# A hybrid transformer step: the ACT queue's gate and rope loads put behind the first modulation weights, parameter loads reordered, one matmul dropped

## The chip, the cores and the metric

The kernel runs on one core of a Trainium2 chip. Its engines are TensorE (PE, with its weight loads shown as PEld), VectorE (DVE), ScalarE (ACT), GpSimd (POOL) and SyncE (SP); SP, ACT and POOL issue the DMA transfers, each on a queue of its own (q1 is SP's, q10 is ACT's, q0 is POOL's), and 16 DMA engines carry them. The metric is the device time of one execution in microseconds, as the median of several runs.

## The reference, cut to what matters

One inference step of a layer: 512 latent tokens and 128 context tokens with 1,024 features pass through an adaptive layer norm (modulation), one input projection, attention beside a gated linear recurrence (RG-LRU), an output projection and a mixture of 32 experts. The change touches the start of it only:

```python
def adaln(cvec, w, b):
    m = jax.nn.silu(cvec) @ w + b            # w: 1024 x 6144
    return six vectors: sh1, sc1, g1, sh2, sc2, g2

h = modulate(rms_norm(x, norm1), sh1, sc1)   # needs the first 2048 columns of w
z = h @ w_in                                 # q, k, v, xr (recurrence), gb (gelu gate)
xc = dw_conv(xr, conv_w, conv_b)             # width 4
r = sigmoid(xc @ wa[d] + ba[d])              # block-diagonal, 8 blocks of 64, two directions
i = sigmoid(xc @ wx[d] + bx[d])
# q and k are normed (q_norm, k_norm) and turned with rotary tables
```

## The kernel before

The program is written by hand, engine by engine: each engine has one list of instructions in order, and semaphores tie the lists together. No scheduler moves anything.

**Start.** SP issues the two conditioning vectors (line 352), the five blocks of tokens (line 354), and then, all on q1, in this order: the first halves of the columns of the eight row blocks of the first 2,048 columns of w_mod (`w_mod_columns(c, 0)`, line 358), a first part of w_in (`w_in(0)`, line 374), the second halves (`w_mod_columns(c, 1)`), `w_in(1)`, and, each behind a wait on PE's progress, `w_mod(8)` to `w_mod(11)` (line 363), `w_in(2)` and `w_in(3)`, four parts of the q/k/v columns (line 392), and `w_mod(12)` onwards. The pieces that a transfer is cut into have the length of a contiguous run: 2 KB for the halves of w_mod, 1 KB for the parts of w_in, 8 KB for `w_mod(8)` and later ones, 3 KB for the q/k/v columns.

**ACT at the start.** It loads the identity, three small parameters (norm1, conv_b, the first 2,048 entries of b_mod), waits for `par_c` and computes a tanh for SiLU, loads five more small parameters into rows of `prow` (tile q_hi_lo), squares the five token blocks for the RMS norm (line 527), loads b_mod for later groups (line 531), evicts transposed tokens (line 540), and then issues 13 transfers in a row: eight of the gate weights (line 554, 64 partitions x 4 runs of 64 floats each, so 256 runs of 256 bytes), two rotary tables (lines 556, 557), q_norm and k_norm broadcast to all partitions (lines 558, 559) and cached values (line 560). Its next work is `z_evict(0)` (line 574), which copies the first 128 recurrence columns out of PSUM.

**PE at the start.** Small warming matmuls (line 1410), `first_modulation(c, half)` (line 1397), the transpose of the parameter rows, which waits for all eight parameter loads (`par_in`, line 1413), and the transposes of the tokens (line 1373); then `mod_turn(0)` (line 1406), a single matmul of the identity whose result nobody reads (line 1425), and the projection `z(m, part)` (line 1464) in two halves of the contraction, because the second half needs the second halves of the modulation. The order from there is: z(0) first half, first_modulation(0,1) and (2,1), z(1,0) first half, first_modulation(4,1) and (6,1), z(1,1) first half, mod_turn(1), z(0) second half, modulation(8) and (9) (line 1385), z(1) second half, gates(0) (line 1439), modulation(10) and (11), z(2) and gates(1), z(3)..., gates(2), modulation(12) and (13), and so on. `gates(0)` waits for all eight gate loads (`gate_in`) and for `conv(0)` on DVE.

**DVE there.** modulate(1), then `conv(0)` (lines 936 and 938, waits for ACT's `z_evict(0)`), `rope_tables()` (lines 982 and 985, waits for the four transfers of `attn_in`, the tables and the two norms), `conv(1)`, `gates(0)` and `gates(1)` of the recurrence (lines 947 to 952), `conv(2)`.

The semaphore `wm_in[5]` counts the second halves of row blocks 4 to 7; at 64 all four have landed. PE waits for it before first_modulation(4,1).

Of the kernel before, what the change touches and what calls it, by code (L numbers as in the profile page):

```python
# [7 lines left out]
ACT = mybir.ActivationFunctionType  # L8
# [8 lines left out]
P = 128  # L17
# [33 lines left out]
WIDE = 4 * 512  # L51
# [14 lines left out]
R_CTX, R_C, R_N1, R_CB, R_CW, R_BA, R_BX, R_LAM, R_ST, R_BM, ROWS = 0, 8, 16, 24, 28, 44, 52, 60, 68, 76, 92  # L66

C_SSQ, C_RSTD, C_HALF, C_TH, C_KAP, C_BA, C_BX, C_LRU, C_MS2, C_RS2, C_KAP2 = 0, 5, 10, 20, 36, 44, 52, 60, 100, 105, 110
# [8 lines left out]
def build(nc, a):  # L77

    with ExitStack() as ctx:
        def sb(name, shape, dt=F32, c=ctx):  # L80
            return c.enter_context(nc.sbuf_tensor(name, shape, dt))

        def sem(name):
            return ctx.enter_context(nc.semaphore(name))


        X = sb("x_tok", [P, NT, D])
        HM = sb("hT_mixT", [P, DC, TOK])
        ident = sb("ident", [P, P])
        par = sb("par_cols", [P, ROWS])  # L90
        mcol = sb("mod_cols", [P, 2, 2, DC])
        csil = sb("silu_c", [P, DC, 32])
        small = sb("small", [P, N_SMALL])
# [12 lines left out]
        final = sb("final_step", [P, 1], U32)  # L106
        count = sb("count_ones", [P, 2, P], F16)
        tab = sb("routing_table", [P, sum(n for _, n in TABLE)])
        logit = sb("logits", [P, NT, NG + NE])
        W1 = sb("w1", [P, DC * D])  # L110
# [41 lines left out]
        ps = ctx.enter_context(nc.psum_tensor("ps", [P, 8, 512], F32))  # L152
# [9 lines left out]
        prow = qhl[:, 0, :]  # L162
# [22 lines left out]
        def temp(c, lo, n):  # L185

            return HM[:, NT + c, lo:lo + n]
# [11 lines left out]
        runs, reps, start = temp(2, 40, NE), temp(2, 72, PAIRS), temp(2, 88, PAIRS + 1)  # L199
# [47 lines left out]
        wm_in = [sem(f"wm_in{i}") for i in range(6)]  # L247
# [262 lines left out]
        def _(act):  # L510
# [1 line left out]
            rows = lambda v: v.rearrange("(c p) -> c p", p=P)  # L512
            act.dma_start(ident[:, :], a["k_ident"]).then_inc(S["ident_in"], 16)

            for v, r in ((a["norm1"][0], R_N1), (a["conv_b"][0], R_CB), (a["b_mod"][0, 0:WIDE], R_BM)):
                n = v.shape[0] // P
                act.dma_start(prow[r:r + n, :], rows(v)).then_inc(S["par_in"], 16)
            act.wait_ge(S["par_c"], 1)
            act.activation(small[:, C_TH:C_TH + 16], par[:, 0:16], ACT.Tanh, scale=0.5).then_inc(S["csil"], 1)
            for v, r in ((a["conv_w"][0], R_CW), (a["lru_ba"][0], R_BA), (a["lru_bx"][0], R_BX),  # L520
                         (a["lru_lambda"][0], R_LAM), (a["state_lru"][0, 0], R_ST)):
                n = v.shape[0] * v.shape[1] // P
                act.dma_start(prow[r:r + n, :], v.rearrange("k (c p) -> (k c) p", p=P)).then_inc(S["par_in"], 16)

            for t in range(NT):
                act.wait_ge(rows_in[t], 16)
# [17 lines left out]
            def mod_out(g):  # L544

                act.wait_ge(S["mod_ev"], g + 2)
                for v in range(2):
                    act.dma_start(a["mod_rows"][v, g * WIDE:(g + 1) * WIDE].rearrange("(q n) -> q n", q=4),
                                  msb[v:v + 97:32, :]).then_inc(S["mod_out"], 16)
            act.wait_ge(S["cleared"], 4)  # L550
            for k, w in enumerate((a["lru_wa"][0], a["lru_wx"][0])):
                for d in range(2):
# [73 lines left out]
            for m in range(1, LC):  # L626
                gates(2 * m - 1)
                z_evict(m + 1)
                roots(m - 1)
                gates(2 * m)  # L630
            mod_out(1)
            z_evict(LC + 1)
            gates(UNITS - 1)
# [4 lines left out]
            q_out(0)  # L638
            squares(2)
            mod_out(2)  # L640
            q_out(1)
            squares(3)
# [11 lines left out]
            for n in range(N + 8):  # L654
# [7 lines left out]
                if n < N:  # L662
                    if n >= 3:
# [3 lines left out]
                                   scale=SCALE, bias=sm[:, 1, n:n + 1], accum_out=sm[:, 2, n:n + 1]).then_inc(S["prob"], 1)  # L667
# [695 lines left out]
        def _(pe):  # L1363
# [38 lines left out]
            def mod_turn(half):  # L1402

                pe.wait_ge(S["mod_ev"], half + 1)
                for b in range(4):
                    ins = pe.matmul(ps[:, 7, 4 * b:4 * b + 4], msb[:, b * P:(b + 1) * P], pairsum, start=True, stop=True)
                ins.then_inc(S["mrow_t"], 1)
# [14 lines left out]
            first_modulation(6, 0)  # L1422
            x_turn(4)
            mod_turn(0)
            pe.matmul(ps[:, 5, :], ident[:, :], X[:, 0, 0:512], start=True, stop=True)

            def gates(u):
                m, d = u // 2, u % 2
# [128 lines left out]
            for n in range(N + 7):  # L1557
# [19 lines left out]
                if n < N:  # L1577
# [6 lines left out]
                    for lo, k, bank in ((0, HALF, b), (HALF, HALF, b + 1)) if t < LT else ((KEYS, CTX, b),):  # L1584
                        for s in range(2):
                            ins = pe.matmul(ps[:, bank, 0:k], qs[:, h, t * P:(t + 1) * P], ks[:, g, s, lo:lo + k],  # L1586
                                            start=(s == 0), stop=(s == 1))
# [13 lines left out]
                if 0 <= m < N:  # L1601
# [6 lines left out]
                    for i in ((0, 1), (2,), (3,), (4,))[part]:  # L1608
                        if i not in kt:
                            continue  # L1610
                        for e in range(2):
# [4 lines left out]
                                            start=(i == 0), stop=(i == kt[-1]))  # L1616
# [73 lines left out]
            for t in range(NT):  # L1690
                for k in range(TOP):
                    ins = pe.matmul(ps[:, 4, 0:COLS], slotp[:, t, k, :], hit[:, t, k, :],
                                    start=(t == 0 and k == 0), stop=(t == NT - 1 and k == TOP - 1))
# [58 lines left out]
            for t in range(NT):  # L1752
                for k in range(TOP):
                    ins = pe.matmul(ps[:, 5, 0:PARTS * COLS], slot1[:, t, k, :],
                                    step1w[:, t * TOP + k, :, :].rearrange("p s n -> p (s n)"),
                                    start=(t == 0 and k == 0), stop=(t == NT - 1 and k == TOP - 1))
# [25 lines left out]
            for t in range(NT):  # L1782
# [4 lines left out]
                for half in range(2):  # L1787
                    if t in PE_SUMS:
                        pe.matmul(ps[:, 2 * t % 8 + half, :], ident[:, :], y0[:, t, half * 512:(half + 1) * 512],
                                  start=True, stop=False)  # L1790
# [63 lines left out]
```

## Time and profile before

| | us |
|---|---|
| median of 3 runs | 632.55 |
| runs | 631.70, 632.55, 633.89 |
| the profiled execution | 631.70 |
| its span, first to last instruction | 629.5 |
| PE busy in it | 595.7 (95%) |
| DVE busy | 352.2 (56%) |
| ACT busy | 177.5 (28%) |
| POOL busy | 94.4 (15%) |
| DMA q1 / q10 / q0, share of 16 engines | 63.1% / 2.4% / 7.1% |

The span is what the profile shows of the execution; the rest of its time lies around it. Busy shares are averages over very different stages: in the first 70 us the DMA engines are busy without a break and PE is fed by them, from 80 to 370 us PE sets the pace, and the experts (from 370 us on) share it between PE and the stream of expert weights.

### The profile page before, as it was taken

To read this page: it belongs to the slowest core of one execution; us is meant where nothing else is said; L and a number is where in the kernel's file an instruction comes from. 1 tells how busy PE (TensorE), PEld (TensorE's weight loads), DVE (VectorE), ACT (ScalarE), POOL (GpSimd) and SP (SyncE) were. 2 spreads that over 40 slices of the span, in tenths; PEclk is the share of its full clock that TensorE was granted. 3 is DMA by queue.
4 is the path that set the end of the run, shared out by engine and by line. 5 is a ranking of instruction groups with operands and counts; after the bars stand their busy time and mean duration, and the time that the engine had idled before them with its cause. 6 is when DMAs were issued, how large, how long until landed. Compare 5 with 4: busy or idle time off the path is not lost.

```text
span 629.5 us, 9459 instructions
## 1 busy us (share of the span) xinstructions
PE 595.7 (95%) x3311; PEld 332.8 (53%) x3312; DVE 352.2 (56%) x786; ACT 177.5 (28%) x369; POOL 94.4 (15%) x131
## 2 busy tenths in 40 slices
PE   4989999999998999999999989999999999789797
PEld 2534455555666677645555445555555555355453
DVE  2747798765664887655666773333334333313347
ACT  4203887601144777721111101100110110011110
POOL 4000011122161000000000111212122121201200
PEclk9999999999999999999999899999999999979999
DMA  8999833330039639539114949999999999999877
GB/s 320 369 363 382 321 148 134 140 133 2 0 89 281 242 95 278 222 107 394 67 68 173 383 172 389 420 418 416 421 418 413 417 421 421 418 423 415 357 261 290
DMA packets 48129, 176.23 MB, mean 280 GB/s; under 512 B 10972, under 2 KB 18152, under 8 KB 34400
## 3 DMA queue, kind: packets, MB, share of 16 engines
q1 hardware_dynamic: 36848, 154.86, 63.1%
q0 software_dynamic: 6688, 15.58, 7.1%
q10 hardware_dynamic: 4560, 5.35, 2.4%
q8 instruction: 21, 0.34, 0.2%
q14 instruction: 12, 0.10, 0.0%
HBM read 163.31 MB, written 21.14 MB: 293 GB/s over the span
## 4 chain that ended last, share of the span: by engine, by line
PE 73%; DMA 13%; SPq 7%; DVE 4%; issue 1%; ACT 1%; POOL 1%; POOLq 0%; DVEq 0%; ACTq 0%
PE ps L1731 16%; PE ps L1548 11%; PE ps L1464 9%; PE ps L1747 7%; PE ps L1476 6%; DMA expert_w<-exp_w_up 5%; PE ps L1586 4%; PE ps L1613 4%; SPq L358 3%; PE ps L1595 3%; DMA w_mod_ring<-w_mod 2%; SPq L329 2%; DMA w<-w_mod 2%; PE ps L1439 2%; PE ps L1699 2%; PE ps L1385 2%
## 5 line engine op out<-in xcount | busy, mean ns | idle before, releaser
L1731 PE MATMUL ps<-expert_w,hT_mixT 128*64 128x256 f32 x1120 | 136.2, 393 | 11.4 <-DMA expert_w<-exp_w_up 11.1
L1731 PEld LDWEIGHTS ps<-expert_w,hT_mixT 128*64 128x64 f32 x1120 | 84.2, 136 | 66.8 <-issue 22.9
L1464 PE MATMUL ps<-hT_mixT,w 128*128 128x128 f32 (+1 forms) x256 | 72.6, 437 | 1.2 <-DVE hT_mixT L913 1.2
L1548 PE MATMUL ps<-w,hT_mixT 128*128 128x512 f32 x160 | 71.9, 597 | 0.0
L1747 PE MATMUL ps<-expert_w,w 128*64 128x512 f32 x280 | 65.8, 598 | 0.0
L736 ACT ACTIVATE w<-ps 128x128 f32<-128x128 f32 x36 | 10.0, 278 | 193.0 <-PE ps L1731 193.0
L1299 DVE SCALAR_TENSOR_TENSOR w<-w,ps 128x128 f32<-128x128 f32 x36 | 10.4, 288 | 86.7 <-ACT w L736 86.7
L1464 PEld LDWEIGHTS ps<-hT_mixT,w 128*128 128x128 f32 x256 | 38.9, 191 | 35.8 <-issue 32.6
L1317 DVE TENSOR_TENSOR w<-ps,w 128x1024 f32<-128x1024 f32 x18 | 22.1, 1225 | 59.9 <-PE ps L1747 59.9
L1476 PE MATMUL ps<-w_qkv,hT_mixT 128*128 128x512 f32 (+1 forms) x160 | 53.2, 488 | 0.2 <-DVE v_tok L1001 0.2
L1548 PEld LDWEIGHTS ps<-w,hT_mixT 128*128 128x128 f32 x160 | 29.1, 191 | 29.9 <-issue 29.7
L1476 PEld LDWEIGHTS ps<-w_qkv,hT_mixT 128*128 128x128 f32 x160 | 29.8, 190 | 22.1 <-issue 19.7
L1747 PEld LDWEIGHTS ps<-expert_w,w 128*64 128x64 f32 x280 | 19.0, 136 | 33.0 <-issue 30.8
L1077 DVE TENSOR_REDUCE softmax_stat<-ps 128x1 f32<-128x640 f32 (+1 forms) x40 | 28.6, 716 | 11.9 <-PE ps L1586 11.8
L1586 PE MATMUL ps<-k_stack,q_stack 128*128 128x320 f32 (+1 forms) x144 | 30.6, 331 | 3.2 <-ACT q_work L666 3.2
L829 POOL DMA_INDIRECT y_rows<-w,slot_row_now x17 | 23.9, 1407 | 55.9 <-DVE w L1317 53.3
L1586 PEld LDWEIGHTS ps<-k_stack,q_stack 128*128 128x128 f32 x144 | 21.2, 188 | 16.7 <-issue 11.5
L666 ACT ACTIVATE q_work<-ps,softmax_stat 128x640 f32<-128x640 f32 (+1 forms) x40 | 28.3, 708 | 4.3 <-DVE softmax_stat L1078 3.9
L661 ACT ACTIVATE w_qkv<-ps 128x640 f32<-128x640 f32 (+1 forms) x40 | 24.7, 618 | 14.5 <-PE ps L1595 14.2
L813 POOL DMA_INDIRECT w<-h_rows,slot_token_now x17 | 17.6, 1033 | 66.7 <-PE ps L1699 66.7
L1613 PE MATMUL ps<-w_qkv,v_tok 128*64 128x256 f32 x168 | 25.6, 400 | 0.0
L1595 PE MATMUL ps<-ident,q_work 128*128 128x128 f32 x168 | 25.2, 275 | 0.0
(287 smaller groups left out, 767.7 us busy)
## 6 DMA issues: line engine op xcount, KB each, us to landing
expert_w<-exp_w_down SPq DMA_DIRECT2D x31, 1024.0 KB, 19.2
expert_w<-exp_w_gate SPq DMA_DIRECT2D x29, 1024.0 KB, 14.8
expert_w<-exp_w_up SPq DMA_DIRECT2D x29, 1024.0 KB, 17.5
w_mod_ring<-w_mod SPq DMA_DIRECT2D x14, 1024.0 KB, 6.5
y_rows<-zero_rows POOLq DMA_DIRECT2D x10, 512.0 KB, 10.0
expert_w<-y_rows SPq DMA_DIRECT2D x10, 512.0 KB, 8.9
recurrence<-w_mod SPq DMA_DIRECT2D x8, 512.0 KB, 10.0
w<-w_in SPq DMA_DIRECT2D x4, 1024.0 KB, 16.7
```

The source lines that it names most:

```text
L661: act.activation(probT[:, m % HEADS, 0:k], wide[:, 4 * 512:4 * 512 + k], ACT.Copy).then_inc(S["pT_a"], 1)
L666: act.activation(probs(n), scores(n), ACT.Exp, scale=SCALE, bias=sm[:, 1, n:n + 1], accum_out=sm[:, 2, n:n + 1]).then_inc(S["prob"], 1)
L829: pool.indirect_dma_start(a["y_rows"], bass.IndirectOffsetOnAxis(pidc[:, 0:1], 0), y, None, bounds_check=TOP * TOK - 1, oob_is_err=False). ...
L1077: step(dve.tensor_reduce(sm[:, 0, n:n + 1], scores(n), AXY, ALU.max))
L1464: ins = pe.matmul(ps[:, bank, 0:n], w1v[:, c, m * P:(m + 1) * P], HM[:, c, lo:lo + n], start=(c == 0), stop=(c == DC - 1))
L1476: ins = pe.matmul(ps[:, bank, 0:n], HM[:, c, t * P:(t + 1) * P], wqv[:, c, lo:lo + n], start=(c == 0), stop=(c == DC - 1))
L1548: ins = pe.matmul(ps[:, 2 * (t % 2) + half, :], HM[:, c, t * P:(t + 1) * P], w1v[:, c, half * 512:(half + 1) * 512], start=(c == 0), stop= ...
L1586: ins = pe.matmul(ps[:, bank, 0:k], qs[:, h, t * P:(t + 1) * P], ks[:, g, s, lo:lo + k], start=(s == 0), stop=(s == 1))
L1595: ins = pe.transpose(ps[:, 4 + i // 4, (i % 4) * P:(i % 4 + 1) * P], prob[:, m % 3, i * P:(i + 1) * P], ident[:, :])
L1613: ins = pe.matmul(out.rearrange("p (b n) -> p b n", b=2), vt[:, i if t < LT else NT, g * HD:(g + 1) * HD], probT[:, 4 * g + e:4 * g + 4:2, ...
L1731: ins = pe.matmul(ps[r, 2 + k, 0:2 * P].rearrange("p (k f) -> p k f", k=2), xT[:, c, r], gate_up(i)[:, :, c, k:FF:FC], start=(c == 0), sto ...
L1747: ins = pe.matmul(ps[r, 5 + half, :].rearrange("p (a n) -> p a n", a=4), actT[:, c, r], down(i, c, half), start=(c == 0), stop=(c == FC - 1))
```

## The change

On ACT, the wait for `par_c` and the tanh come ahead of all parameter loads but the identity, and the 16 rows of b_mod come last of the eight parameter loads. Also on ACT, a wait for `wm_in[5]` to reach 64 is put ahead of the 13 transfers of gates, tables, norms and cached values. On PE, the single unread matmul behind `mod_turn(0)` is gone.

```diff
             act.dma_start(ident[:, :], a["k_ident"]).then_inc(S["ident_in"], 16)
 
-            for v, r in ((a["norm1"][0], R_N1), (a["conv_b"][0], R_CB), (a["b_mod"][0, 0:WIDE], R_BM)):
+            act.wait_ge(S["par_c"], 1)
+            act.activation(small[:, C_TH:C_TH + 16], par[:, 0:16], ACT.Tanh, scale=0.5).then_inc(S["csil"], 1)
+            for v, r in ((a["norm1"][0], R_N1), (a["conv_b"][0], R_CB)):
                 n = v.shape[0] // P
                 act.dma_start(prow[r:r + n, :], rows(v)).then_inc(S["par_in"], 16)
-            act.wait_ge(S["par_c"], 1)
-            act.activation(small[:, C_TH:C_TH + 16], par[:, 0:16], ACT.Tanh, scale=0.5).then_inc(S["csil"], 1)
             for v, r in ((a["conv_w"][0], R_CW), (a["lru_ba"][0], R_BA), (a["lru_bx"][0], R_BX),
                          (a["lru_lambda"][0], R_LAM), (a["state_lru"][0, 0], R_ST)):
                 n = v.shape[0] * v.shape[1] // P
                 act.dma_start(prow[r:r + n, :], v.rearrange("k (c p) -> (k c) p", p=P)).then_inc(S["par_in"], 16)
+            act.dma_start(prow[R_BM:ROWS, :], a["b_mod"][0, 0:WIDE].rearrange("(r p) -> r p", p=P)).then_inc(S["par_in"], 16)
...
+            act.wait_ge(wm_in[5], 64)
             act.wait_ge(S["cleared"], 4)
             for k, w in enumerate((a["lru_wa"][0], a["lru_wx"][0])):
...
             mod_turn(0)
-            pe.matmul(ps[:, 5, :], ident[:, :], X[:, 0, 0:512], start=True, stop=True)
```

ACT's list at the very start, before (q_hi_lo is the tile of the parameter rows, the names behind the arrow are the inputs; what an instruction waits for stands in brackets):

```order
L513 DMA ident<-k_ident 128x128
L517 DMA q_hi_lo<-norm1 8x128
L517 DMA q_hi_lo<-conv_b 4x128
L517 DMA q_hi_lo<-b_mod 16x128
L519 ACT_TABLE_LOAD
L519 ACTIVATE small<-par_cols 128x16 [waits par_c]
L523 DMA q_hi_lo<-conv_w 16x128
L523 DMA q_hi_lo<-lru_ba 8x128
L523 DMA q_hi_lo<-lru_bx 8x128
L523 DMA q_hi_lo<-lru_lambda 8x128
L523 DMA q_hi_lo<-state_lru 8x128
L527 ACTIVATE w_qkv,small<-x_tok 128x1024 [waits rows_in0]
```

The same place on ACT with the change:

```order
L513 DMA ident<-k_ident 128x128
L516 ACT_TABLE_LOAD
L516 ACTIVATE small<-par_cols 128x16 [waits par_c]
L519 DMA q_hi_lo<-norm 8x128
L519 DMA q_hi_lo<-conv_b 4x128
L523 DMA q_hi_lo<-conv_w 16x128
L523 DMA q_hi_lo<-lru_ba 8x128
L523 DMA q_hi_lo<-lru_bx 8x128
L523 DMA q_hi_lo<-lru_lambda 8x128
L523 DMA q_hi_lo<-state_lru 8x128
L524 DMA q_hi_lo<-b_mod 16x128
L528 ACTIVATE w_qkv,small<-x_tok 128x1024 [waits rows_in0]
```

Three loads moved from ahead of the tanh to behind it, b_mod to the end, all of them still ahead of the first square.

ACT's list at the 13 transfers, before (gate_w, rope, gain and v_tok are their tiles; xr_pad is what `z_evict` writes):

```order
L540 ACTIVATE hT_mixT<-ps 128x4x128 [waits xnT] x5
L554 DMA gate_w<-lru_wa 64x4x64 [waits cleared]
L554 DMA gate_w<-lru_wa 64x4x64 x3
L554 DMA gate_w<-lru_wx 64x4x64 x4
L556 DMA rope<-k_cos 128x256
L557 DMA rope<-k_sin 128x256
L558 DMA gain<-q_norm 128x64
L559 DMA gain<-k_norm 128x64
L560 DMA v_tok<-cache_v 128x128
L574 ACTIVATE xr_pad<-ps 128x512 [waits z_mm,cleared]
```

And with the change:

```order
L541 ACTIVATE hT_mixT<-ps 128x4x128 [waits xnT] x5
L556 DMA gate_w<-lru_wa 64x4x64 [waits cleared,wm_in5]
L556 DMA gate_w<-lru_wa 64x4x64 x3
L556 DMA gate_w<-lru_wx 64x4x64 x4
L558 DMA rope<-k_cos 128x256
L559 DMA rope<-k_sin 128x256
L560 DMA gain<-q_norm 128x64
L561 DMA gain<-k_norm 128x64
L562 DMA v_tok<-cache_v 128x128
L576 ACTIVATE xr_pad<-ps 128x512 [waits z_mm,cleared]
```

The order is the same; the first of the 13 now waits for wm_in5 too, and the other twelve and the eviction of xr_pad stand behind it.

## Rows read from the trace of the kernel before

**Rows 1.** Chain of work that ended last, 0 to 60 us: start, us, what.

```profile
24.30 13.91 DMA w<-w_mod
38.26 1.92 PE ps L1397 x16
...
58.16 14.30 DMA w_mod_ring<-w_mod
```

**Rows 2.** Timeline of PE, 24 to 73 us: start, us, line, shapes, [idle before <-releaser].

```profile
24.99 1.10 PE L1425 MATMUL ps<-x_tok,ident 128*128 128x512 f32 x2
26.27 4.56 PE L1464 MATMUL ps<-hT_mixT,w 128*128 128x512 f32 x16 [0.17 <-DVE hT_mixT L913]
38.26 1.06 PE L1397 MATMUL ps<-w_mod_ring,silu_c 128*32 128x512 f32 x8 [1.66 <-DMA w<-w_mod]
53.92 2.33 PE L1439 MATMUL ps<-xc,gate_w 128*128 128x512 f32 x8
72.50 1.06 PE L1385 MATMUL ps<-w_mod_ring,silu_c 128*32 128x512 f32 x8 [0.23 <-DMA w_mod_ring<-w_mod]
```

**Rows 3.** Timeline of ACT at its 13 transfers (ACTq: issuing) and z_evict(0).

```profile
24.33 2.69 ACTq L554 DMA_DIRECT2D gate_w<-lru_wa x4
27.05 3.80 ACTq L554 DMA_DIRECT2D gate_w<-lru_wx x4
30.88 1.57 ACTq L556 DMA_DIRECT2D rope<-k_cos x1
...
35.74 0.45 ACTq L560 DMA_DIRECT2D v_tok<-cache_v x1
46.91 0.60 ACT L574 ACTIVATE xr_pad<-ps 128x512 f32<-128x512 f32 x1 [21.99 <-PE ps L1464]
```

**Rows 4.** DMA queues, 28 to 36 us: packets, MB, share of 16 engines.

```profile
q10 hardware_dynamic: 1187, 0.29, 17.3%
```

**Rows 5.** DMA queues, 37 to 40 us.

```profile
q10 hardware_dynamic: 727, 0.18, 29.7%
```

**Rows 6.** DMA queues, 42 to 48 us.

```profile
q1 hardware_dynamic: 316, 2.33, 94.3%
q10 hardware_dynamic: 316, 0.15, 9.0%
```

**Rows 7.** DMA queues, 52 to 56 us.

```profile
q1 hardware_dynamic: 1356, 1.39, 108.5%
```

**Rows 8.** Tile gate_w: its two groups of issues, and all eight to landing.

```profile
L554 ACTq DMA_DIRECT2D gate_w<-lru_wx x4: 637/638/1797, 27.0 to 29.0; - x4
DMA to landing us min/median/max: 6.6/10.9/13.1
```

**Rows 9.** Tile gain: q_norm and k_norm, us from issue to landing.

```profile
DMA to landing us min/median/max: 14.8/15.7/16.6
```

**Rows 10.** Timeline of DVE, 48 to 68 us.

```profile
48.05 0.80 DVE L936 TENSOR_SCALAR xc<-xr_pad,par_cols 128x512 f32<-128x512 f32 x2 [2.60 <-ACT xr_pad L574]
52.04 0.43 DVE L982 TENSOR_TENSOR rope_k<-rope,gain 128x256 f32<-128x256 f32 x1
...
59.46 0.83 DVE L947 SCALAR_TENSOR_TENSOR q_work<-recurrence 128x640 f32<-128x640 f32 x1 [1.00 <-ACT recurrence L593]
67.07 0.82 DVE L947 SCALAR_TENSOR_TENSOR q_work<-recurrence 128x640 f32<-128x640 f32 x1 [5.19 <-ACT recurrence L593]
```

**Rows 11.** Windows: us, busy of PE, PEld, DVE, ACT, POOL, PEclk, DMA share, GB/s.

```profile
15.00:18.00 3.00, 3.00 (x15) 1.28 (x14) 2.87 (x6) 0.75 (x3) 0.00 (x0) 0.50 1.06 363
36.00:38.00 2.00, 0.60 (x2) 0.00 (x0) 0.00 (x0) 0.00 (x0) 0.00 (x0) 1.00 1.12 317
```

**Rows 12.** Timeline of ACT and PE, 5 to 15 us.

```profile
5.34 1.06 ACT L527 ACTIVATE w_qkv<-x_tok 128x1024 f32<-128x1024 f32 x1 [1.34 <-DMA x_tok<-x_sample]
10.77 1.06 ACT L527 ACTIVATE w_qkv<-x_tok 128x1024 f32<-128x1024 f32 x1
13.58 1.06 PE L1397 MATMUL ps<-recurrence,silu_c 128*32 128x512 f32 x8 [3.45 <-DMA recurrence<-w_mod]
```

## The prediction, on record before the change was run

> **What bounds the kernel now.** I read the chain of waits first. In the first 60 us it is fed by transfers: the last first-modulation matmuls start when the second halves of w_mod have landed at 38.26, and the next link that is a transfer is `w_mod(13)`, which takes the chain from 58.16 to 72.5 [rows 1]. PE's timeline says what each is worth: PE stood idle 1.66 us before 38.26 and 0.23 us before 72.50, and in between no other wait for a transfer is listed for it; it came to gates(0) at 53.92 and went straight on [rows 2]. From 72.5 to the end of attention PE lists no wait for a transfer, so a delay of PE there goes through to the end almost whole.
>
> Then the DMA queues by stretch. q1 (SP) and q10 (ACT) share the 16 engines, and they take turns piece by piece: from 42 to 48 us, when q1 carries the 8 KB pieces of w_mod(8) and later, both moved 316 pieces, 53 per us [rows 6]. When q1 carries 2 KB pieces, q10 gets 1,187 in 8 us, 148 per us [rows 4]; with the 1 KB pieces of w_in it gets 727 in 3 us, 242 per us [rows 5]. Alone, q1 moves 1,356 pieces of 1 KB in 4 us, 339 per us [rows 7]. So how fast ACT's small transfers get through is set by how long SP's pieces are at that moment. That decides this case.
>
> **The start of ACT (tanh first, b_mod last).** The tanh can come some 0.4 us earlier, but its reader, first_modulation, waits for w_mod until 13.58 [rows 12]: worth nothing. The three loads that moved behind it take about 1.2 us of issuing, so the first square starts near 6.6 instead of 5.34. The squares were held by token arrivals, so the last one moves from 10.77 by about 0.3 us only, and the normed tokens come 0.3 us later. PE waits for w_mod again right after the first transposes, and that absorbs it. b_mod's parameter rows would be issued near 6.4; with the 6.6 us of the quickest gate load [rows 8] they land by 13.0, ahead of PE's need at 14.64, where its first modulation ends [rows 12]. Cost 0; if that cover is gone, 0.3 us.
>
> **The unread matmul (line 1425).** With its group it takes 1.10 us at 24.99, and z(0) behind it waits for DVE's modulate until 26.27 anyway [rows 2]. Gain 0 to 0.1 us. It kept PE busy, so the clock is the risk: but the idle 1.66 us before 38.26 left the granted clock at 1.00 [rows 11], and the hole here would be 1.2 us. Taken as 0.
>
> **The wait for wm_in[5]: what it gives.** q10 held 17.3% of the engines over the 8 us from 28 to 36 [rows 4], 1.4 us, and some 0.1 more until the halves of w_mod were through. Without it they land near 38.26 - 1.5 = 36.8, and PE, free at 36.6, goes on 1.5 us earlier: first_modulation(4,1), z(0), modulation(8), (9) and z(1) all move up, and PE reaches gates(0) near 52.4.
>
> **What it costs, first the gate weights.** The 13 issues start at 36.8 instead of 24.33. The quickest gate load took 6.6 us to landing [rows 8], of which its 256 pieces and some 16 closing ones are 1.8 us at 148 per us [rows 4]; so beside a busy q1 the first piece moves some 4 us or a little more after the issue, here at about 41. What is q1 doing then? Behind the halves come the 1,024 pieces of w_in(1): at 339 per us, 3 us, they are through by about 38. Then come the 4 MB of w_mod(8) to (11) in 8 KB pieces, at 2.33 MB in 6 us [rows 6] 10 to 10.5 us, to about 48.5. In those 7.5 us q10 moves 7.5 x 53 = 400 pieces. The eight gate loads are 8 x 256 = 2,048 pieces and some 16 closing ones each, 2,176. The remaining 1,780 go beside the 1 KB pieces of w_in(2) and (3), at 242 per us: 7.3 us, to 55.8. With the last landing they are there at about **56.5**. In the run before they had a landing time of at most 13.1 us [rows 8] from issues that ended at 30.85 [rows 3], so were there by 42.
>
> **Second, ACT itself.** ACT needs its own list: z_evict(0) stands behind the 13 issues. Before, they took from 24.33 to 36.2, 11.9 us, and z_evict(0) was at 46.91, right when PE delivered [rows 3]. The first seven gate issues took 0.64 us each, the eighth 1.80 [rows 8], the tables 1.57 and about 1.4, the last 0.45 [rows 3]. I read this as a queue that takes no more than a certain stock: when the eighth was issued, from 29.0 to 30.85, seven had put 1,904 pieces in, and by my rate of 148 per us from 28.5 on some 75 of them had been moved at 29.0 and some 350 at 30.85. Lower bound: the same 11.9 us, ACT free at 48.7. Upper bound: the same stock, about 1,540 pieces before a new issue goes in; then the eighth issue waits until some 370 are moved (48), and the last until about 1,200 are moved (400 by 48.5, then 242 per us: 51.8), ACT free at 52.3. conv(0) follows the eviction (46.91 to 52.04 [rows 3, 10], 5.1 us), so it ends between 53.8 and **57.4**. I take the upper one, since it is the reading that explains the growing issue times.
>
> PE waits for both at gates(0). Two separate roads give 56.5 and 57.4; I take 57.2, against 53.92: +3.3 us. At 72.5 PE no longer waits for w_mod(13), whose bytes are the same in either program: -0.2. The 1.5 us won at 38 is inside this: it is lost at gates(0), and would be lost at 72.5 otherwise.
>
> **Third, the clock.** PE would be idle from 52.4 to 57.2, 4.8 us. After the idle 3.45 us before 13.58 [rows 12] the granted clock was 0.50 from 15 to 18 [rows 11], in all some 3.4 us at the lower of its two levels (1.2 instead of 2.4 GHz). Work at that level loses half of its time: at most 1.7 us for one such stretch, none if it passes while PE still waits. I take 1.2.
>
> **Fourth, DVE.** q_norm and k_norm took 14.8 and 16.6 us to land [rows 9]. Now the four transfers of attn_in are 576 pieces behind the gates: near 60. DVE waits there in rope_tables, its own 2 us and conv(1) (4 us, as conv(0) [rows 10]) bring it to 66, and DVE's gates(0) moves from 59.46 to there. But before its next one DVE had 5.19 us idle at 67.07 [rows 10], and its need moves by 4 us as well: gates(1) near 71 finds DVE free at 68.5, and PE wants conv(1) only at gates(2), near 73. Taken as 0; bound 2 us.
>
> Sum: +3.3 - 0.2 + 1.2 = **+4.3 us** on the profiled execution: span 629.5 to 633.8, its time 631.70 to 636.0. The profiled one is 0.85 us under the median of the runs, so the median goes from 632.55 to **636.9**.
>
> **Rivals.** (a) Late, but mildly: ACT gets through in its old 11.9 us, the gate loads alone hold PE to 56.5, and the clock doesn't fall in work: +2.6 - 0.2 = +2.4, 635.0. For it: ACT's slow issues fell into a time in which SP's were held up too, so they may not count stock at all.
> (b) In time, and absorbed: q10 gets several small pieces for each long one of q1. With nine for one, 53 x 9 = 477 per us, 2,176 pieces would be through in 4.6 us, landed by 47; ACT is free by 45, PE runs through at 52.4 and then waits 1.7 us at 72.5 for w_mod(13). Change about 0, 632.4. Against it: 316 to 316. The Trainium skill (DMA: Bandwidth & Descriptors, section Queues, rings and completion order) says that an engine drains a whole packet, typically nine to seventeen descriptors, from one ring before it turns to the next. By that rule this rival would be the outcome; the counts of pieces here speak against it.
> (c) Faster: as (b), and w_mod(13) lands earlier too. Its mechanism is the tail of q1's stream: SP issues w_mod(12) and (13) on PE's progress (57 to 58), and if the landing at 72.5 hangs on the issue and not on the bytes ahead, all 1.5 us go through: 631.0. Against it: 14.3 us from issue to landing [rows 1] is a queue of bytes.
> (d) Much later, beyond 639.5: q10 starts later than 41, the clock falls twice, or DVE's delay reaches gates(2).
>
> **How the numbers follow.** Forecast 0.50 (635.3 to 639.5), (a) 0.17, (b) 0.17, (c) 0.07, (d) 0.09. From 632.0 to 639.5 lie the forecast, (a) and most of (b), 0.82. A change within 0.3%, 1.9 us, is about what a measurement can't tell from none. Slower by more: the forecast, (d) and most of (a), 0.73. Same: (b) and the rest of (a), 0.20. Faster: 0.07.
>
> **What would show it.** Right: PE starts first_modulation(4,1) at 36.6 to 37; the issues of the gate loads begin there and the last of the 13 ends near 52; z_evict(0) at 52 instead of 46.9; gates(0) on PE near 57, with a wait of 4 to 5 us for ACT/DVE or a gate load; granted clock 0.5 for some us behind it; DVE waiting for gain near 60; no wait at modulation(13). Wrong: q10 moving far more pieces per us than q1 between 41 and 48, or z_evict(0) at 45.4. If gates(0) starts by 54.5, the forecast falls.

## The result, and the profile after

| | before | changed |
|---|---|---|
| median, us | 632.55 (630.50 to 635.09, 6 runs) | 637.81 (637.21 to 638.93, 6 runs) |
| ratio, 95% interval | | 1.0083 [1.0057, 1.0108] |
| profiled execution, us | 631.70 | 639.40 |
| its span | 629.5 | 637.4 |

The changed kernel is 5.3 us slower. Its profiled execution lies 1.6 us above its own median, so its rows show a little more than the change costs; the kernel was run once more later, beside three of the experiments: 636.80 us, 1.0077 [1.0050, 1.0105].

ACT's timeline of the changed kernel, 24 to 55 us (start, us, line, tiles, and in brackets the idle time before and what ended it), answers to [rows 3]:

```profile
37.53 2.68 ACTq L556 DMA_DIRECT2D gate_w<-lru_wa  x4
40.24 9.56 ACTq L556 DMA_DIRECT2D gate_w<-lru_wx  x4
49.83 0.79 ACTq L558 DMA_DIRECT2D rope<-k_cos  x1
...
52.66 0.49 ACTq L562 DMA_DIRECT2D v_tok<-cache_v  x1
53.25 0.77 ACT L576 ACTIVATE xr_pad<-ps 128x512 f32<-128x512 f32 x2 [26.53 <-DMA w_mod_ring<-w_mod]
```

The 13 issues take 15.6 us for 11.9 before. The last four gate issues take 5.8 us more than before, all of it in two of them, and the five issues behind them 2.0 us less. z_evict(0), at 46.91 before, is at 53.25. The chain of waits shows the two issues apart, and what follows them (start, us, what):

```profile
25.07 12.44 DMA w<-w_mod
...
40.91 3.05 ACTq L556
43.99 5.02 ACTq L556
49.03 10.13 DMA gate_w<-lru_wx
59.21 4.03 PE ps L1440 x8
```

In [rows 1] the path runs from w_mod's halves into PE's own work; now it runs through ACT's issues into the landing of the last gate load. PE's timeline, beside [rows 2]:

```profile
28.08 6.26 PE L1465 MATMUL ps<-hT_mixT,w 128*128 128x512 f32 x16 [1.14 <-DVE hT_mixT L915]
39.75 1.07 PE L1399 MATMUL ps<-w_mod_ring,silu_c 128*32 128x512 f32 x8
50.98 4.59 PE L1465 MATMUL ps<-hT_mixT,w 128*128 128x512 f32 x16
59.21 4.03 PE L1440 MATMUL ps<-xc,gate_w 128*128 128x512 f32 x8 [3.64 <-DMA gate_w<-lru_wx]
78.22 1.92 PE L1387 MATMUL ps<-w_mod_ring,silu_c 128*32 128x512 f32 x16
```

gates(0) starts 5.3 us later than at 53.92, takes 4.03 in place of 2.33 us, and the 0.23 us of waiting for w_mod(13) is gone: 5.3 + 1.7 - 0.2 = 6.8 us in this execution. The 1.7 us are the granted clock (us, busy of PE, PEld, DVE, ACT, POOL, PEclk, DMA share, GB/s):

```profile
60.00:63.00 3.00, 3.00 (x7) 1.44 (x5) 0.41 (x1) 0.79 (x1) 0.00 (x0) 0.50 1.04 394
```

z(0)'s first half took 6.26 us here for 4.56 before, at the lower clock too; gates(0) waited for its loads all the same, so that loss is not added.

The spans differ by more, 7.9 us, and a second reading tells what of that lies at the start. When the 304 ACTIVATE instructions of ACT are matched in order with those of before, they come later by the same amount all the way from 122 to 355 us, within 0.05 us. This **lag behind before** is 6.6 us in this profile and 5.0 us in the second profile of the changed kernel. What the spans differ by beyond it arises after 355 us, in single executions, and is not put down to the change.

### The profile page after: what moved, and what is told of

Read it like the earlier page. It is cut to its first block, busy times and chain, and to the rows that moved or that the text cites. A ratio compares the mean times of both kernels' runs of the same rounds, so it can differ in the third digit from the quotient of the medians.

```text
span 637.4 us, 9456 instructions
## 1 busy us (share of the span) xinstructions
PE 597.0 (94%) x3309; PEld 332.6 (52%) x3310; DVE 352.5 (55%) x786; ACT 177.2 (28%) x369; POOL 94.6 (15%) x131
## 4 chain that ended last, share of the span: by engine, by line
PE 71%; DMA 11%; SPq 7%; DVE 5%; ACTq 2%; issue 2%; ACT 1%; POOL 1%; POOLq 0%; DVEq 0%
PE ps L1732 16%; PE ps L1549 11%; PE ps L1465 8%; PE ps L1748 7%; PE ps L1477 5%; DMA expert_w<-exp_w_up 5%; PE ps L1587 4%; PE ps L1614 4%; PE ps L1440 3%; SPq L358 3%; PE ps L1596 3%; SPq L329 2%; PE ps L1700 2%; DMA w<-w_mod 2%; ACTq L556 2%; DMA gate_w<-lru_wx 2%
## 5 line engine op out<-in xcount | busy, mean ns | idle before, releaser
L1465 PE MATMUL ps<-hT_mixT,w 128*128 128x128 f32 (+1 forms) x256 | 74.3, 444 | 2.2 <-DVE hT_mixT L915 2.2
L1079 DVE TENSOR_REDUCE softmax_stat<-ps 128x1 f32<-128x640 f32 (+1 forms) x40 | 28.6, 716 | 11.9 <-PE ps L1587 11.9
```

The costliest lines, as they stand in the source:

```text
L1079: step(dve.tensor_reduce(sm[:, 0, n:n + 1], scores(n), AXY, ALU.max))
L1465: ins = pe.matmul(ps[:, bank, 0:n], w1v[:, c, m * P:(m + 1) * P], HM[:, c, lo:lo + n], start=(c == 0), stop=(c == DC - 1))
```

## The experiments

Each kernel was run in five rounds beside the kernel before; ratios are to it, with 95% intervals, and can differ by some 0.1% from the quotient of two medians. The median of before was 632.83 us for the four kernels of the first section below, 633.32 for the two that ask for the road, the one on the clock and the first with the gate loads on SP, and 632.29 for the other four.

### One edit of the change at a time

The wait alone:

```diff
+            act.wait_ge(wm_in[5], 64)
             act.wait_ge(S["cleared"], 4)
```

> The kernel before with nothing but ACT's wait for the second halves of w_mod ahead of its 13 transfers. My theory: the wait alone makes the change's whole loss of some 5 us. gates(0) on PE starts 4 to 5.5 us later than in before, behind a gate load whose issue is held until about 49, and runs at the lower clock; time +3.5 to +5.5 us. Rival 1: the parameter loads at the start carry a part (the changed kernel's tokens landed 1.8 us later than before's), then this is only +2 to +3.5 us. Rival 2: the unread matmul carries a part by the clock (z(0) took 6.26 us instead of 4.56 in the changed kernel), then also +2 to +3.5 us and z(0) takes 4.6 us here.

Measured: 637.94 us, 1.0078 [1.0048, 1.0108]. The wait alone makes the whole loss; its lag behind before is 4.9 us. ACT and PE in it, and the DMA queues from 40 to 45 us (packets, MB, share of 16 engines):

```profile
39.28 8.51 ACTq L555 DMA_DIRECT2D gate_w<-lru_wx  x4
```

```profile
57.41 4.12 PE L1440 MATMUL ps<-xc,gate_w 128*128 128x512 f32 x8 [3.81 <-DMA gate_w<-lru_wx]
```

```profile
q1 hardware_dynamic: 267, 1.97, 97.3%
q10 hardware_dynamic: 228, 0.06, 5.6%
```

From 43 to 45 us it was 99 pieces to 98. Equal counts over microseconds could also come from turns of many pieces on either queue. But they are equal in quarters of a microsecond as well, 16 to 16, 10 to 10, 10 to 11 and 15 to 14 from 41 to 42 us, and an 8 KB piece holds one of the 16 engines some 0.3 us (96.4% of the 16 engines for 51 such pieces in this microsecond). By that estimate nine in a row would keep an engine from q10 for 2.7 us. z_evict(0) is at 51.49.

The order of ACT's start alone (the pieces of the change up to b_mod, shown with it above, without the wait and with the unread matmul kept):

```diff
+            act.wait_ge(S["par_c"], 1)
+            act.activation(small[:, C_TH:C_TH + 16], par[:, 0:16], ACT.Tanh, scale=0.5).then_inc(S["csil"], 1)
...
+            act.dma_start(prow[R_BM:ROWS, :], a["b_mod"][0, 0:WIDE].rearrange("(r p) -> r p", p=P)).then_inc(S["par_in"], 16)
```

> The kernel before with only the start of ACT's list changed: tanh first, norm1 and conv_b behind it, b_mod last. My theory: nothing that can be measured, -0.5 to +0.7 us, since PE waits for w_mod anyway; the first squares start near 7 and the last token block is squared at most 0.5 us later. Rival: the loads collide with the tokens and w_mod, so that tokens land 1 to 2 us later, first_modulation starts near 15.4 instead of 13.6 and z(0) near 28 instead of 26.3; as PE's next wait for a transfer at 38.26 has only 1.66 us in it, up to 0.3 us of that go through, or more if the whole stream of w_mod is later: +0.5 to +2.

Measured: 634.39 us, 1.0024 [0.9998, 1.0050]; not told apart from nothing, and a loss of up to 0.5% not excluded. What the profile shows is a later start of the squares, which the issues ahead of them cause, and PE still waiting for w_mod:

```profile
6.61 1.06 ACT L528 ACTIVATE w_qkv<-x_tok 128x1024 f32<-128x1024 f32 x1 [3.00 <-issue]
10.78 1.04 ACT L528 ACTIVATE w_qkv<-x_tok 128x1024 f32<-128x1024 f32 x1
```

```profile
13.28 1.07 PE L1398 MATMUL ps<-recurrence,silu_c 128*32 128x512 f32 x8 [1.40 <-DMA recurrence<-w_mod]
```

The unread matmul left out alone:

```diff
-            pe.matmul(ps[:, 5, :], ident[:, :], X[:, 0, 0:512], start=True, stop=True)
```

> The kernel before without the single unread matmul behind mod_turn(0). My theory: 0 us (within 0.5), z(0) starts at the same time and takes 4.6 us at the higher clock. Rival: PE's hole of 1.2 us before z(0) lets the granted clock fall to 0.5 during z(0), which then takes 6.3 us instead of 4.6; of these 1.7 us the idle 1.66 us before 38.26 takes most: +0 to +1 us.

Measured: 632.54 us, 0.9997 [0.9973, 1.0020]. PE waits for DVE 1.14 us where the matmul was, and z(0) starts at 25.68: no cost is shown.

All three edits, but with the wait behind the eight gate loads, so that only tables, norms and cached values wait:

```diff
-            act.wait_ge(wm_in[5], 64)
             act.wait_ge(S["cleared"], 4)
...
+            act.wait_ge(wm_in[5], 64)
             act.dma_start(rope[:, 0, :, :], a["k_cos"]).then_inc(S["attn_in"], 16)
```

> The changed kernel with its wait moved down, behind the eight gate loads and ahead of the tables, the norms and the cached values. My theory: what costs is the gate loads' late landing, not the wait as such; here they are issued near 24.5 and landed by 42 as in before, the five later issues go out at 37.5 to 41 without being held, z_evict(0) is on time, and gates(0) starts at 53 to 54.5: time within 1 us of before. The tables then land by 50 to 53 and DVE waits for them 0 to 2 us, which costs nothing. Rival: ACT's list is what counts, and any issues behind the wait are held by SP's until about 49 to 52: z_evict(0) comes 2 to 5 us late and the time is +2 to +5 us.

Measured: 633.43 us, 1.0011 [0.9989, 1.0032]. The five late transfers are issued without any hold, and gates(0) does not wait:

```profile
38.34 0.36 ACTq L558 DMA_DIRECT2D rope<-k_cos  x1
40.16 0.46 ACTq L562 DMA_DIRECT2D v_tok<-cache_v  x1
```

```profile
43.21 6.29 PE L1465 MATMUL ps<-hT_mixT,w 128*128 128x512 f32 x16 [1.05 <-DVE hT_mixT L915]
55.71 2.33 PE L1440 MATMUL ps<-xc,gate_w 128*128 128x512 f32 x8
```

Its gates(0) is 1.8 us later than before, and 1.7 us of that are z(0)'s second half, which ran at the lower clock (6.29 in place of 4.59 us). So what costs is the delay of the gate loads, not that of the tables.

### Which road holds gates(0): ACT's list or the gate loads

With the wait alone, the five issues of tables, norms and cached values moved behind z_evict(0):

```diff
-            act.dma_start(rope[:, 0, :, :], a["k_cos"]).then_inc(S["attn_in"], 16)
...
             z_evict(0)
+            act.dma_start(rope[:, 0, :, :], a["k_cos"]).then_inc(S["attn_in"], 16)
...
```

> As x_wait_only (the kernel before plus the wait), with z_evict(0) moved up in ACT's list, between the eight gate loads and the five later ones. My theory: the eighth gate load's landing (57.4 there) holds gates(0); ACT's late eviction (51.5 there) is the second, hidden cause. So z_evict(0) comes near 47.8, conv(0) ends near 53, and gates(0) still starts near 57: time as x_wait_only, +4 to +5.5 us against before. Rival: ACT's list is the cause, then gates(0) starts 2 to 4 us earlier, +1 to +3 us.

Measured: 637.31 us, 1.0063 [1.0037, 1.0089]. The eviction came 3.6 us earlier than with the wait alone, and gates(0) didn't:

```profile
47.91 0.60 ACT L570 ACTIVATE xr_pad<-ps 128x512 f32<-128x512 f32 x1 [23.49 <-PE ps L1465]
```

```profile
57.48 2.43 PE L1440 MATMUL ps<-xc,gate_w 128*128 128x512 f32 x8 [3.40 <-DMA gate_w<-lru_wx]
```

With the wait alone, SP's `w_in(2)` and `w_in(3)` held until PE has done modulation(9), so that SP issues nothing while ACT's sixth and seventh issue are held:

```diff
+            modulation_done(DC + 1)
             w_in(2)
-            modulation_done(DC + 1)
```

> As x_wait_only, with SP's w_in(2) and w_in(3) issued only after modulation(9), near 49, where the q/k/v columns are issued. It asks what held ACT's seventh and eighth gate issue (until 47.8 in x_wait_only): theory A, SP's issues of w_in(2) and (3), each of 1,024 pieces, stand before ACT's on a path that both share; then all 13 issues take 0.4 to 0.7 us each here, ACT is free by 45.5, the gates land by 50, gates(0) starts at 51.5 to 54, and the time is within 2 us of before. Theory B, my prediction's: q10 takes only a certain stock of pieces; then the seventh and eighth issues are held as before until pieces have been moved, to 44 or later, whatever SP does. The expert stream and the rest are untouched in both; w_mod(13) may land up to 2 us later, since q1 runs out of work near 48 for a moment.

Measured: 636.39 us, 1.0041 [1.0022, 1.0061]. ACT's issues were held as with the wait alone (8.30 us for 8.51), and now ACT's list is the later road: the last gate load landed at 53.6, and gates(0) waited for conv(0) behind z_evict(0):

```profile
39.41 8.30 ACTq L555 DMA_DIRECT2D gate_w<-lru_wx  x4
...
51.80 1.43 ACT L575 ACTIVATE xr_pad<-ps 128x512 f32<-128x512 f32 x4 [27.19 <-PE ps L1465]
```

```profile
56.70 3.94 PE L1440 MATMUL ps<-xc,gate_w 128*128 128x512 f32 x8 [4.17 <-DVE xc L939]
```

Together: the landing of the gate loads holds gates(0) at 57.4, and ACT's list, if that road were free, at 56.7. By the profiles, mending one of them alone gains at most 0.7 to 0.8 us. The medians of this kernel and of the one with the wait alone lie further apart (1.0041 and 1.0078), but their intervals overlap.

### What the clock costs

The changed kernel with four unread matmuls of the identity ahead of gates(0), so that PE works while it waits:

```diff
+            for _ in range(4):
+                pe.matmul(ps[:, 5, :], ident[:, :], X[:, 0, 0:512], start=True, stop=True)
```

> The changed kernel with four unread matmuls on PE ahead of gates(0), 3.4 us of work where PE is idle. My theory: 1.2 to 1.7 us of the loss is the clock. gates(0) starts where it did (59.2 in that profile) but takes 2.3 us instead of 4.0, and the time is 1 to 1.7 us under the changed kernel's, +3.3 to +4.3 us against before. Rival: the clock falls all the same or its loss is made good elsewhere; then no difference to the changed kernel.

Measured: 635.07 us, 1.0027 [1.0009, 1.0045], against 1.0077 and 1.0083 for the changed kernel. PE and the clock windows:

```profile
57.43 2.43 PE L1440 MATMUL ps<-xc,gate_w 128*128 128x512 f32 x8 [1.65 <-DMA gate_w<-lru_wx]
```

```profile
57.00:60.00 3.00, 2.57 (x12) 1.44 (x16) 0.00 (x0) 0.90 (x2) 0.00 (x0) 1.00 1.06 374
60.00:63.00 3.00, 3.00 (x19) 0.94 (x12) 1.94 (x6) 2.94 (x4) 0.00 (x0) 1.00 1.04 395
```

gates(0) starts where it does with the wait alone and in the second profile of the changed kernel (57.41, 57.71) and runs at full clock. The profiles give 4.03 - 2.43 = 1.6 us, and the lag behind before is 3.2 us, for 4.9 with the wait alone and 5.0 in that second profile: 1.7 to 1.8 us for the clock. The difference of the ratios is 0.5%, 3.2 us, and the cost against before, 1.7 us, is under the 3.3 to 4.3 that were expected; but each ratio carries 1 to 2 us of uncertainty, and no profile shows more than the 1.8 us. This kernel's own profiled execution took 637.15 us, 2.1 above its median: from 359 to 365 us its granted clock was 0.50.

### Why the gate loads and ACT's issues are so slow

The wait alone, and w_mod(8) to (11) each in two transfers of 2 KB pieces in place of one of 8 KB pieces; the bytes and the order of the row blocks on q1 are the same:

```diff
+                if n < DC + 4:
+                    for half in range(2):
+                        sp.dma_start(w_mod_place(n)[:, half::2, :],
+                                     wmod_v[n // DC, n % DC].rearrange("p (q n) -> p q n", q=4)[:, half::2, :]).then_inc(here, 16)
+                    return
```

> The kernel before with the wait of the change alone, and w_mod(8) to w_mod(11) each sent as two transfers in pieces of 2 KB in place of one in pieces of 8 KB. Tells apart what holds ACT's sixth and seventh gate-load issue. Theory: SP's queue and ACT's are served piece for piece, so that ACT's queue moves only some 50 pieces per us beside 8 KB pieces; beside 2 KB pieces it moves about 150 per us from 41 us on, ACT's ring empties sooner, the sixth and seventh issue are held at most 2 us each (before the change 0.4 and 1.6 us), ACT has issued its last table by 46 us, and gates(0) starts between 55.5 and 57 us by the landing of the gate loads; time 635 to 637.5 us. Rival: what holds the issues is not the pace of ACT's queue: they are held to about 47.8 us as with the wait alone, gates(0) starts at 57.4 or later and the time is 637.5 to 639 us.

Measured: 633.63 us, 1.0018 [1.0001, 1.0036]: 0.6% of the 0.8% are gone with the length of SP's pieces, more than was expected (635 to 637.5 us); the lag behind before is 0.7 us for 4.9. DMA queues from 40 to 45 us, ACT, and PE:

```profile
q1 hardware_dynamic: 827, 1.59, 91.8%
q10 hardware_dynamic: 677, 0.17, 15.7%
```

```profile
36.51 2.69 ACTq L560 DMA_DIRECT2D gate_w<-lru_wa  x4
39.24 3.42 ACTq L560 DMA_DIRECT2D gate_w<-lru_wx  x4
...
48.25 0.77 ACT L580 ACTIVATE xr_pad<-ps 128x512 f32<-128x512 f32 x2 [23.93 <-issue]
```

```profile
54.41 2.43 PE L1445 MATMUL ps<-xc,gate_w 128*128 128x512 f32 x8 [2.06 <-DMA gate_w<-lru_wx]
```

q10 moves three times as many pieces in the same stretch (677 to 228), the issues take 3.42 in place of 8.51 us, and gates(0) starts 3.0 us earlier, still behind the landing of the gate loads. Beside 2 KB pieces q10 again moved as many pieces as q1, 160 to 162 from 41 to 42 us. The last landing follows the pace of q10; that far the theory is confirmed, and gates(0) at 54.41 came earlier than the 55.5 to 57 expected. For the held issues it is so only in part. With the wait alone the sixth issue is held from 39.95 us on, when q10 had not moved a piece in either kernel (its first ones are from 40 to 41 us, 19 and 39 of them), and with 2 KB pieces the sixth and seventh go through at 39.91 and 40.58. So the length of SP's pieces decides whether ACT is held there, but not by way of what q10 has moved by then. Before the change the sixth and seventh issue took 0.64 us each, not the 0.4 and 1.6 us that the expectation names.

### The changed kernel again, and two tries to beat the kernel before

> The changed kernel once more, beside the other three. By the first measurement of it 4 to 6 us slower than before (636.8 to 638.8 us), gates(0) between 57 and 59.3 us in its profile behind the landing of the gate loads, with a stretch at 1.2 GHz in the first gates. If gates(0) starts near 57.4 here, the extra 1.8 us of the first profile was its own and not the change's.

Measured: 636.80 us, 1.0077 [1.0050, 1.0105]. Its PE:

```profile
38.04 1.06 PE L1399 MATMUL ps<-w_mod_ring,silu_c 128*32 128x512 f32 x8
57.71 3.97 PE L1440 MATMUL ps<-xc,gate_w 128*128 128x512 f32 x8 [3.85 <-DMA gate_w<-lru_wx]
```

So gates(0) belongs at 57.4 to 57.7, and 1.5 us of the 59.21 in the first profile were that execution's own. There PE was later at 39.75, SP issued w_mod(10) and (11), which wait for PE, at 40.88 only, and from 50 to 53 us q1 moved 706 pieces with 0.91 MB, so some long ones were still among them, beside 280 of q10; the wait alone had 743 beside 740. That this chain made the 1.5 us is argued from the times and was not tried.

If ACT's place is wrong, SP's might be right: the gate loads issued by SP on q1, between the halves of w_mod and `w_in(1)`, which itself came behind w_mod(9), w_mod(12) and (13) ahead of `w_in(3)`, and tables, norms and cached values loaded by ACT only from 77.7 us on, with `rope_tables()` on DVE moved to just ahead of `scans(2)`.

```diff
+            sp.wait_ge(S["cleared"], 4)
+            for k, w in enumerate((a["lru_wa"][0], a["lru_wx"][0])):
+                for d in range(2):
+                    for b in range(2):
+                        sp.dma_start(gw[b * 64:b * 64 + 64, d, k, :, b * 64:b * 64 + 64],
+                                      w[d].rearrange("(m b) i j -> b i m j", b=2)[b]).then_inc(S["gate_in"], 16)
...
+            w_in(1)
...
+            for n in (DC + 4, DC + 5):
+                modulation_done(n - 2)
+                w_mod(n)
```

> A version that follows the change's aim in another way. From before: the eight gate loads are issued by SP on q1 right behind the second halves of w_mod, so that they neither share the engines with them nor wait for a turn against 8 KB pieces; w_in(1) goes behind w_mod(9); w_mod(12) and (13) go ahead of w_in(3) and the q/k/v columns; the tables, norms and cached values are loaded after 73 us and rope_tables runs before scans(2), in DVE's idle time. If the waits at 38.26 (1.66 us) and 72.5 (0.23 us) are what the transfers cost PE there, both shrink: first_modulation(4,1) starts near 36.7, gates(0) near 52.5, no wait at modulation(13): -1 to -1.9 us. Rival: PE gains at 38 and loses it again at modulation(9) or at gates(0) behind a gate load: within 0.5 us of before. A third: DVE's rope_tables lengthens the recurrence's chain, up to +2.

Measured: 631.46 us, 0.9980 [0.9957, 1.0003]; the interval holds 1, so no gain is shown. gates(0) and modulation(12) and (13) run without a wait, but z(0) fell into the lower clock, and gates(0) came at 54.59, not near 52.5:

```profile
42.09 6.29 PE L1468 MATMUL ps<-hT_mixT,w 128*128 128x512 f32 x16 [1.05 <-DVE hT_mixT L916]
54.59 2.33 PE L1443 MATMUL ps<-xc,gate_w 128*128 128x512 f32 x8
71.88 1.92 PE L1389 MATMUL ps<-w_mod_ring,silu_c 128*32 128x512 f32 x16
```

The same with two unread matmuls in the holes of PE near 36 and 41 us, and those two matmuls alone in the kernel before (this line twice, behind the first half of z(1,0) and behind `mod_turn(1)`):

```diff
+            pe.matmul(ps[:, 5, :], ident[:, :], X[:, 0, 0:512], start=True, stop=True)
```

> The kernel with the gate loads issued by SP behind the halves of w_mod (which came out 1.3 us faster than before), plus the same two unread matmuls. Theory: the two gains add, 2 to 3 us faster than before, gates(0) starts at 53.5 to 54.8 us without a wait and no stretch at 1.2 GHz lies between 36 and 60 us. Rival: the clock falls elsewhere or the holes are too long for one matmul each, and it stays within 1.5 us of before.

> The kernel before plus two matmuls whose result is never read, one behind the first half of z(1,0) and one behind mod_turn(1). Theory: they keep the granted clock up over the holes near 36.6 us and 41 to 43 us, which in some executions bring a stretch at 1.2 GHz; 0.3 to 1.5 us faster than before on the median. Rival: the low stretches come at the same places or elsewhere, and the time is within 0.3% of before.

Measured: 630.20 us, 0.9976 [0.9952, 1.0000], with the gate loads on SP, and 632.17 us, 0.9985 [0.9966, 1.0004], with the two matmuls alone. For the first, the profile shows what was hoped for:

```profile
41.76 4.59 PE L1468 MATMUL ps<-hT_mixT,w 128*128 128x512 f32 x16
...
52.56 2.33 PE L1443 MATMUL ps<-xc,gate_w 128*128 128x512 f32 x8
```

gates(0) is 1.4 us earlier than in the kernel before, and from 122 to 355 us the kernel is 1.8 us ahead of it. The runs give 2.1 us less on the median with an interval that ends at 1.0000, so a gain is likely and not shown. For the two matmuls alone no gain is shown.

## Why the prediction was right, step by step

- **What bounds the start** held. From the tokens to gates(0) the kernel is fed by q1 and q10, and the change moved the end of the chain into them.
- **ACT's start, cost 0 (up to 0.3).** The shift of the squares was 1.2 us as worked out, or up to 1.1 us more: they start at 6.54 to 7.60 us in the profiles with that edit, against 5.34 [rows 12], and the last one between 10.7 and 12.6. No cost is shown by the edit alone, 1.0024 with an interval from 0.9998 to 1.0050, and the kernel with all edits but the early wait (1.0011) speaks for less.
- **The unread matmul, 0 to 0.1 us.** No cost is shown, and the clock that it might have cost didn't fall in the profile of that edit. Over all profiles the risk is not gone: of the five without this matmul, z(0)'s first half took 6.26 us in two (the changed kernel's first, and the wait behind the gates) and 4.56 in three; in the nine with it, it took 4.56. Two of five can be chance, and what is lost there can vanish in the wait for w_mod at 38 us.
- **The gain of the wait, 1.5 us at 38.26.** Right where the start of the execution was like before's: with the eviction ahead of the tables PE starts first_modulation(4,1) at 36.57 (0.75 us idle for w_mod), and at 36.52 in the changed kernel with four matmuls more, where 36.8 was forecast. In the two profiles of the changed kernel itself PE came there at 38.04 and 39.75 without waiting, since in both w_mod's first halves had fed PE later (14.39 and 15.36 us for 13.58) and PE then ran for some us at 1.2 GHz. That the executions differ there didn't matter to gates(0) in the first case, where it started at 57.71: the gain and this loss both vanish behind the gate loads.
- **Gate loads, landing at 56.5.** The mechanism held: one piece of q10 for one of q1, about 50 per us beside 8 KB pieces. The rule cited in the prediction for rival (b), from the Trainium skill (DMA: Bandwidth & Descriptors, section Queues, rings and completion order), lets an engine take a whole packet of several descriptors from one ring and then turn to the next. It holds for both queues alike, so it would not have given q10 nine small pieces for one long one, as the prediction reads it; and the equal counts in quarters of a microsecond show turns of about one piece for these transfers, shorter than the packets that the page calls typical. The size was 0.9 us short. With the wait alone q10's first piece moved at 40.5, for 41 forecast. It moved 228 pieces from 40 to 45 us, 593 more by 50, 740 by 53 and 872 by 57, so its 2,176 pieces were through near 55.8, as worked out; the last landing came at 57.4, 1.6 us behind, not 0.7. A load has landed when its semaphore has had 16 increments; 13 of the last load's came by 56.2 and the others at 56.80, 56.89 and 57.37. So the tail is that of a few late increments, and what makes those late was not tried.
- **ACT's list, free at 52.3 by the stock.** The number came out (z_evict(0) at 51.5 to 51.8 in four profiles, 53.25 in the first of the changed kernel), the reading behind it did not, so this agreement is luck. It was the sixth and seventh gate issue that were held, not the eighth and the last. With 2 KB pieces seven transfers of 256 pieces were put in with at most some 80 moved; beside 8 KB pieces the sixth was held with five put in. No one stock of q10's pieces explains both. What the runs show is that the hold hangs on the length of SP's pieces, and not on SP's issue of w_in(2), since ACT was held for the same time without that issue. What in an issue waits is open.
- **Two roads, 57.2.** Both roads exist and lie close, but the other way round: gate loads 57.4, ACT 56.7, for 56.5 and 57.4. The maximum of the two, 57.2 for 57.4 to 57.7 measured, hid the exchange; that too is luck.
- **-0.2 at 72.5.** Right: no wait at modulation(13).
- **Clock, +1.2 (up to 1.7).** The stretch fell wholly into work: 3.97 to 4.12 for 2.33 us in gates(0), in both profiles of the changed kernel and in that of the wait alone, 1.6 to 1.8 us. The upper bound would have been the better value, since PE's hole ended with gates(0) and the clock fell just then. It did not fall in every profile: with the eviction ahead of the tables PE was idle 3.40 us before gates(0), which then took 2.43 us, and the lag behind before is 3.2 us there.
- **DVE, 0.** Right. DVE waited for gain (first profile of the changed kernel):

```profile
62.59 0.43 DVE L984 TENSOR_TENSOR rope_k<-rope,gain 128x256 f32<-128x256 f32 x1 [4.58 <-DMA gain<-k_norm]
68.81 0.82 DVE L949 SCALAR_TENSOR_TENSOR q_work<-recurrence 128x640 f32<-128x640 f32 x1
74.09 0.82 DVE L949 SCALAR_TENSOR_TENSOR q_work<-recurrence 128x640 f32<-128x640 f32 x1 [2.86 <-ACT recurrence L595]
```

The tables came at 62.6, the first step of the recurrence at 68.8 instead of 66, and 2.86 of the 5.19 us of idle time in [rows 10] were left.

The sum of +4.3 us stands against 5.2 worked out in the same way from the second profile (57.71 - 53.92 = 3.8, 1.6 for the clock and -0.2), a lag behind before of 5.0 us in it, and 4.5 and 5.3 us between the medians. What was missing is part of the tail of the landing and the rest of the clock. Rival (a) underrates both roads; (b) and (c) fall with the 1:1 count; (d) with q10's start at 40.5 and the time.

## What to carry to other kernels

Two queues on the same DMA engines here took turns by pieces, so the pace of a transfer in small pieces is set by the length of the other queue's pieces at that moment: before delaying a small load to make room for a large one, look which pieces it will then share the engines with. A delayed issue also takes its engine's list with it; work out both the landing and the time at which the engine comes free, and expect that mending one alone gains little. A hole in PE of 3.6 to 4.2 us was paid twice in four profiles here, by itself and by 1.6 to 1.8 us at the lower clock behind it. And where single executions differ by as much as the change is worth, matching the same instructions of two profiles over a long stretch tells the one from the other: the lag here was constant from 122 to 355 us, and what came on top later belonged to the execution.

## What was not expected of the hardware

- A DMA issue on ACT, 0.64 us otherwise, lasted 3 to 5 us twice in a row beside 8 KB pieces on the other queue; beside 2 KB pieces none of the eight gate issues took over 1.5 us. SP's own issues of w_in(2) and (3) took 7.99 us for the two with the 2 KB pieces, 8.38 in the kernel before and 4.73 with the wait alone, so they are held as well, and not by the length of the pieces alone.
- The hole that precedes a fall of the clock doesn't tell whether it falls. After 2.40 us of idle time before first_modulation(4,1) it stayed up (the unread matmul left out), after 2.17 us it fell (the order of ACT's start), and after two holes of 0.94 and 1.05 us it fell as well (the wait behind the gates). Further on it fell from 357 to 359 us in the kernel before and not in the one without the unread matmul. That moves single executions of all these kernels by 1.7 us a time, about the size of the differences that were looked for among them.
